# First mixer of a two-block transformer kernel: value products, selection rounds, a late sigmoid and the second output slab in another order

## The reference, cut to what matters

```python
def mixer(u, w_in, w_uk, w_uv, w_up_a, w_up_b, w_o, pos, topk):
    proj = u @ w_in                      # cut into qa ka va qb ckv krope qi ki wi ga gb
    y_a = stick_breaking(qa, ka, va)     # 8 heads: scores, log-keep sums over later keys, exp, times v
    ...
    # dsa_attention, 8 heads:
    s_idx = relu(einsum('bqhd,bkd->bqhk', qi, k_idx))       # index products
    score = einsum('bqh,bqhk->bqk', wi, s_idx)
    _, sel = lax.top_k(score, topk)                          # topk = 64 keys of each query
    p = softmax(logits of the selected keys);  y_b = p @ values
    z = sigmoid(ga) * (y_a @ w_up_a) + sigmoid(gb) * (y_b @ w_up_b)
    return z @ w_o
```

## Time and profile before

| what | value |
|---|---|
| median of 3 runs | 1602.22 us (1595.94 to 1602.30) |
| profiled execution | 1602.0 us, span 1600.2 us |
| TensorE busy | 1411.3 us, 88% |
| VectorE busy | 725.9 us, 45% |
| ScalarE busy | 522.0 us, 33% |
| GpSimd busy | 168.4 us, 11% |
| HBM read | 357.70 MB, 224 GB/s over the span |
| first mixer, from the last input slab to the last `wo` unit | about 141 to 292 us |
| expert stage | about 320 to 740 us |

### The profile page before, as it was taken

One profiled execution on the slowest core, in us unless ns is written; L12 is line 12 of the kernel. 1 busy time (PEld: TensorE's weight loads), 2 busy tenths in 40 slices (PEclk: granted clock), 3 DMA queues, 4 the chain that ended last, 5 costly groups with the idle time before them and its releaser, 6 DMA issues.

```text
span 1600.2 us, 27601 instructions
## 1 busy us (share of the span) xinstructions
PE 1411.3 (88%) x11842; PEld 1185.5 (74%) x11842; DVE 725.9 (45%) x1221; ACT 522.0 (33%) x798; POOL 168.4 (11%) x145
## 2 busy tenths in 40 slices
PE   5999888897676776776899997999999999999997
PEld 5999557764344444443697997999999887799997
DVE  4345465431121111111675566565646664566544
ACT  4354444210010000000524444344344433454442
POOL 2000002200000000000200003311124300111122
PEclk7999799798888888887899998999999999999998
DMA  7340113799999999999534540444345331354450
GB/s 310 130 189 8 73 54 139 300 410 428 428 428 429 428 428 429 428 430 427 199 143 172 211 170 3 158 182 187 114 177 210 132 145 53 127 190 171 150 180 28
DMA packets 31988, 359.98 MB, mean 225 GB/s; under 512 B 5280, under 2 KB 8352, under 8 KB 9632
## 3 DMA queue, kind: packets, MB, share of 16 engines
q1 hardware_dynamic: 31904, 358.76, 56.1%
HBM read 357.70 MB, written 1.05 MB: 224 GB/s over the span
## 4 chain that ended last, share of the span: by engine, by line
PE 68%; DMA 19%; DVE 5%; ACT 4%; issue 2%; POOL 2%; SPq 1%; ACTq 0%; DVEq 0%
PE PS L508 41%; DMA expert_w<-in_w 19%; PE PS L521 5%; PE PS L954 4%; PE PS L568 3%; PE PS L974 2%; PE PS L926 1%; SPq L387 1%; PE PS L1127 1%; DVE wl L1849 1%; ACT wh L1376 1%; PE PS L808 1%; PE PS L1321 1%; POOL UL L2543 1%; PE PS L665 1%
## 5 line engine op out<-in xcount | busy, mean ns | idle before, releaser
L1849 DVE TENSOR_TENSOR wl<-raw,wh 128x4096 fp32r<-128x4096 f32 (+2 forms) x69 | 281.4, 4078 | 215.0 <-ACT wh L1376 214.9
L1376 ACT ACTIVATE wh<-raw 128x4096 fp32r<-128x4096 f32 (+2 forms) x70 | 233.9, 3341 | 119.2 <-PE PS L508 114.0
L508 PE MATMUL PS<-UH,wh 128*128 128x272 f32 (+1 forms) x840 | 245.8, 293 | 14.0 <-DVE wl L1914 9.6
L954 PE MATMUL PS<-expert_w,XW 128*32 128x256 f32 x2048 | 161.4, 471 | 97.6 <-DMA expert_w<-in_w 97.3
L508 PE MATMUL PS<-UH,wl 128*128 128x272 f32 (+1 forms) x840 | 242.7, 289 | 0.0
L508 PE MATMUL PS<-UL,wh 128*128 128x272 f32 (+1 forms) x840 | 242.2, 288 | 0.0
L954 PEld LDWEIGHTS PS<-expert_w,XW 128*32 128x32 f32 x2048 | 74.4, 130 | 172.9 <-issue 88.6
L508 PEld LDWEIGHTS PS<-UH,wh 128*128 128x128 f32 x840 | 160.3, 191 | 16.2 <-DVE wl L1914 10.0
L508 PEld LDWEIGHTS PS<-UL,wh 128*128 128x128 f32 x840 | 160.8, 191 | 0.4
L508 PEld LDWEIGHTS PS<-UH,wl 128*128 128x128 f32 x840 | 160.5, 191 | 0.0
L2217 DVE TENSOR_TENSOR SG<-PS,SG 128x128 f32<-128x128 f32 x32 | 9.3, 291 | 284.9 <-ACT SG L1620 284.9
(11 more groups left out here) (520 smaller groups left out, 2883.5 us busy)
## 6 DMA issues: line engine op xcount, KB each, us to landing
expert_w<-in_w SPq DMA_DIRECT2D x96, 2048.0 KB, 20.7
raw<-in_up SPq DMA_DIRECT2D x22, 2048.0 KB, 7.8
raw<-in_down SPq DMA_DIRECT2D x16, 1408.0 KB, 6.1
raw<-in_ret_v SPq DMA_DIRECT2D x4, 2048.0 KB, 7.9
raw<-in_ret_gate SPq DMA_DIRECT2D x4, 2048.0 KB, 7.8
raw<-in_ret_o SPq DMA_DIRECT2D x4, 2048.0 KB, 8.5
raw<-in_ret_qk SPq DMA_DIRECT2D x3, 2048.0 KB, 7.8
raw<-in_w_in_ga SPq DMA_DIRECT2D x2, 2048.0 KB, 7.9
```

Of the source, the lines that this page charges most:

```text
L508: mm = pe.matmul(gbank(g)[:, c0:T], w[:, c:c + P], x(k)[:, c0:], start=(k == 0 and j == 0), stop=(k == nk - 1 and j == 2))
L954: mm = pe.matmul(PS[32 * j:32 * j + 32, 5 + s, 0:2 * P], XW[:, 4 * half + k, WIN * s:WIN * s + WIN], XPT[3 * s + half][:, (4 * k + j) * 2 ...
L1376: act.activation(WH[n % 2][:, 0:w], raw(n)[:, 0:w], ACT.Copy).then_inc(hi_done, 1)
L1849: dve.tensor_tensor(wl_of(n)[:, 0:w], raw(n)[:, 0:w], WH[n % 2][:, 0:w].bitcast(F32), ALU.subtract).then_inc(lo_done, 1)
```

## The change

It makes six edits, all in the first mixer:

1. On `pe`, `sb_values(0)` goes ahead of `index_products(HEADS, 4)` and `sb_values(1)` ahead of `index_products(HEADS + 4, 4)`. On `act`, `sb_high` goes ahead of `index_relu` in the same two places, and on `dve` `sb_out` ahead of `index_scores`.
2. On `dve`, six rounds of tile 0 stand between the first two pairs; `key_mask(0)` and four rounds of tile 1 ahead of `sb_softplus(3)`; `sb_out(2)`, four rounds, `key_mask(1)` and `sb_out(3)` behind it.
3. On `act`, the late sigmoid goes ahead of the four pieces of slab 12.
4. `ZT` gets four buffers in place of two, so that `dve` waits for the `ZL` of unit m - 4.
5. Slab 13 is split in four pieces on `act` and `dve`. On `dve` piece 0 stands ahead of `add_to_h(0)` and pieces 1 to 3 behind `UM` of blocks 0 to 2; the `memset` of `ZERO` goes from block 0 to block 3.
6. On `pe`, the units 4, 5 and 6 of `wo` wait for pieces 0, 1 and 2, and unit 7 for the whole slab. The piece counts that the second block waits for grow by three.

```diff
-    ZT = region("ZT", [2, T], 17408)
+    ZT = region("ZT", [4, T], 17408)
@@ pe
             pe.wait_ge(freed["act"], FREED[UNIT0["gb"] + 7][1])
+            sb_values(0)
             index_products(HEADS, 4)
-            sb_values(0)
             sb_later(1)
             sb_scores(2)
+            sb_values(1)
             index_products(HEADS + 4, 4)
-            sb_values(1)
             sb_later(2)
@@ pe
             for n in (12, 13):
-                slab_ready(n)
+                if n == 12:
+                    slab_ready(n)
                 for u in range(4):
                     m = 4 * (n - 12) + u
+                    if 4 <= m < 7:
+                        pe.wait_ge(lo_piece, 9 + u + 1)
+                    elif m == 7:
+                        slab_ready(n)
@@ pe, first_units
-                                pe.wait_ge(lo_piece, 9 + u + 1)
+                                pe.wait_ge(lo_piece, 12 + u + 1)
@@ act
             sb_log(1)
+            sb_high(0)
             index_relu(HEADS, 4)
-            sb_high(0)
             sb_weights(2)
             sb_weights(3)
             sb_log(2)
+            sb_high(1)
             index_relu(HEADS + 4, 4)
-            sb_high(1)
@@ act
+            act.activation(GB[:, 4:8, META:], GB[:, 4:8, META:], ACT.Sigmoid).then_inc(gb_sig, 1)
             for q in range(4):
                 hi_part(12, q)
-            act.activation(GB[:, 4:8, META:], GB[:, 4:8, META:], ACT.Sigmoid).then_inc(gb_sig, 1)
             for m in range(8):
                 act.wait_ge(z_done, m + 1)
-                act.activation(ZH[:, m, META:], ZT[:, m % 2, META:], ACT.Copy).then_inc(z_hi, 1)
-            hi(13)
+                act.activation(ZH[:, m, META:], ZT[:, m % 4, META:], ACT.Copy).then_inc(z_hi, 1)
+            for q in range(4):
+                hi_part(13, q)
@@ dve
             sb_softplus(1)
+            sb_out(0)
             index_scores(HEADS, 4)
-            sb_out(0)
-            for _ in range(3):
+            for _ in range(6):
                 take_best(0)
             sb_softplus(2)
+            sb_out(1)
             index_scores(HEADS + 4, 4)
-            sb_out(1)
-            for _ in range(3):
-                take_best(0)
-            sb_softplus(3)
             dve.wait_ge(dsa_in, 48)
             key_mask(0)
+            for _ in range(4):
+                take_best(1)
+            sb_softplus(3)
             sb_out(2)
-            for _ in range(3):
-                take_best(1)
-            sb_out(3)
-            for _ in range(5):
+            for _ in range(4):
                 take_best(1)
             key_mask(1)
+            sb_out(3)
@@ dve
-                if m >= 2:
-                    dve.wait_ge(z_lo, m - 1)
+                if m >= 4:
+                    dve.wait_ge(z_lo, m - 3)
@@ dve
-            lo(13)
+            lo_part(13, 0)
             for m in range(8):
                 add_to_h(UNIT0["wo"] + m, m, META)
...
-                if m == 0:
+                if m < 3:
+                    lo_part(13, m + 1)
+                elif m == 3:
                     link(dve.memset(ZERO[:], 0.0))
```

More of the change, by code:

```diff
@@ L2081, in _ @@
                     dve.wait_ge(gb_sig, 1)
-                if m >= 2:
-                    dve.wait_ge(z_lo, m - 1)
-                freeing(dve.tensor_tensor(ZT[:, m % 2, META:], gbank(g)[:, META:T], GB[:, m, META:], ALU.mult))
+                if m >= 4:
+                    dve.wait_ge(z_lo, m - 3)
+                freeing(dve.tensor_tensor(ZT[:, m % 4, META:], gbank(g)[:, META:T], GB[:, m, META:], ALU.mult))
                 dve.wait_ge(freed["dve"], FREED[g][1])
-                dve.tensor_tensor(ZT[:, m % 2, META:], ZT[:, m % 2, META:], GA[:, m, META:], ALU.add).then_inc(z_done, 1)
+                dve.tensor_tensor(ZT[:, m % 4, META:], ZT[:, m % 4, META:], GA[:, m, META:], ALU.add).then_inc(z_done, 1)
                 if m < 4:
                     lo_part(12, m)
-            lo(13)
+            lo_part(13, 0)
             for m in range(8):
@@ L2549, in _ @@
                 pool.wait_ge(z_hi, m + 1)
-                pool.tensor_tensor(ZL[:, m, META:], ZT[:, m % 2, META:], ZH[:, m, META:].bitcast(F32), ALU.subtract)\
+                pool.tensor_tensor(ZL[:, m, META:], ZT[:, m % 4, META:], ZH[:, m, META:].bitcast(F32), ALU.subtract)\
                     .then_inc(z_lo, 1)
```

## The result

The changed kernel takes **1580.68 us** (median of 4 runs, 1579.94 to 1584.37) against 1601.03 us for the kernel before, run beside it (4 runs, 1595.94 to 1602.30). The ratio is 0.9894, 95% interval 0.9860 to 0.9927: 1.1% less, some 17 us, where 19 were forecast. The profiled execution took 1584.37 us, with a span of 1582.5 us against 1600.2.

A forecast was written before the change was run, and what follows sets the result against it. TensorE carries 68% of the chain that ended last, so its pauses and the clock falls behind them counted. Terms 6.3 + 4.5 + 1.3 + 7.0 = 19.1 us, from 1602.0 us, gave 1583 us, range 1576 to 1590.

The forecast's parts named there:

- Edits 1 and 2, the order: Head pairs to first DSA maxima: value products earlier and rounds spread win 6.3 us at the clock of before.
- The 3.3 us from the rounds: End of the pairs: with rounds moved earlier, VectorE is no longer last and the maxima follow TensorE's first scores.
- The 3.0 us from the values: Two head-pair pauses: value products move into the pause, net 1.5 us for a pair, twice.
- The clock in the pauses: Two head-pair pauses, shortened to 1.9 us: one of two keeps TensorE's clock, worth 4.5 us, bounds 0 and 8.5.
- The start of the DSA steps: TensorE's pause around the first maxima all but goes, so the first gated unit runs faster: 1.3 us, bounds 0 and 2.
- Edits 3 and 4: Ahead of the output units: the wait for `ZL` goes and the first output units start 1.2 us earlier.
- Edits 5 and 6: Output units: TensorE's 3.15 us wait for `UM` goes, and with it the clock's fall, 2.6 us.
- Does it reach the end?: Expert stage moves as a whole with the chain before it; expert 0's load has over 40 us of lead.
- a loss at the experts: Rival: expert 0's lead or the load order counts, up to 6 us lost, 1589 us; chance 0.08.
- late pieces: Rival: an output unit of 4 to 7 waits for `lo_piece` in place of `UM`, 1589 us; chance 0.04.
- a late `pool`: Rival: GpSimd is last in front of the first output units and the clock falls, 1605 us, slower; chance 0.03.
- The base: Starting time for the whole kernel: the profiled execution's 1602.0 us, taken as the median of 1602.22 within 0.3 us.

The follow-up runs named there:

- the filled dispatch: Changed kernel plus 14 unused products of 256 columns on TensorE ahead of the dispatch products in the routing: 1578.16 us, ratio 0.9877.
- the filled kernel: Changed kernel plus five unused products of 432 columns ahead of the index products of steps 10 and 14 each: 1578.71 us, ratio 0.9878.
- the fully filled one: Changed kernel plus unused products in four TensorE pauses: two in the pairs, ahead of the first turning, and ahead of the dispatch: 1574.51 us, ratio 0.9863.

## Why the prediction was right, point by point

**The total.** 1583 us were forecast, within 1576 to 1590, and 1580.7 came. 19.1 us were to be won, and 17.6 us lie between the two spans. 1.5 us of them passed ahead of pair 1, in a part that the change doesn't touch (scores of pair 1 start at 158.9 instead of 160.5). So the profiles show 16 us of it, and the ratios 0.9894 and 0.9898 also 16 to 17.

**Edits 1 and 2, the order: 6.3 us.** Right in mechanism, and in size at the clock of before. The 3.3 us from the rounds: 12.6 became 9.4 or 9.5 us in every kernel that spreads them, and stayed 12.6 in every one that doesn't; 9.3 were worked out. VectorE's idle time ahead of `sb_softplus(2)` took up the rounds, as forecast: 7.53 us became 2.67. The 3.0 us from the values: the pause measured 1.74 us (1.9 forecast), `sb_high` 0.37 us (0.4 taken), and pair 1 to `sb_later(1)` went from 8.2 to 6.1 or 6.6 us (1.5 forecast). The prediction added the two edits, and the four profiles with neither, one or both show that they do add: 42.6, 39.6, 39.4 and 36.4 us. The size of the values' term hangs on the clock, though: 3.0 us where they ran at the low clock before, 1.6 us with the clock at 1.00 throughout.

**The clock in the pauses: 4.5 us, one of two kept.** Near as a size, too simple as a picture. The weak step is "as 1.9 us lies about midway between 1.35 and 2.64, I take one of the two": the length of the pause doesn't decide it. A pause of 2.64 us kept the clock once, and of the eight pauses of 1.74 us in the four profiles with this order of the pairs and no filler in them (the changed kernel twice, edits 1 and 2 alone, the filled dispatch) two kept it, in the last two kernels, the first pause each time; in both profiles of the changed kernel both pauses lost it. What also differs is how long it stayed low behind a pause: 3.4 and 13.7 us in the first profile of the changed kernel, 3.4 and 3.4 in the second, 10.2 and 6.8 us in the two with one pause kept. Against the 33.0 us of the filled kernel the low clock cost 6.6 and 3.3 us with both lost, 4.4 and 3.3 us with one lost. So a pause has no price that is either 0 or 4.5 us, it has a spread of prices. The pairs moved by 8.0 us in the profiled execution, 10.8 forecast, and by 11.3 with the second one (47.7 - 36.4); that the 10.8 lie between is in part luck. The price with the clock at 1.00 throughout was right to 0.1 us: 32.9 us worked out from the earlier trace rows, 33.0 measured once the pauses were filled. Its two parts were less exact, since the 1.9 us of values ran at the low clock too: of the 14.7 us the clock was worth 9.9 (8.5 worked out) and the order 4.8 (6.3 worked out).

The Trainium skill (TensorE: Matmul & The Clock Gate, "What's actually happening") has two levels for this clock, lifted by activity, and says that the number of slow products at a kernel's start differs from run to run. These runs agree with the two levels, and show such differences behind later pauses too: with unused products in the pause the work that took 1.56 us takes 1.01. But a busy TensorE doesn't always see its clock rise soon. In the changed kernel it worked nearly without a break behind the second pause and still was at 0.50 (columns of the earlier trace rows):

```profile
186.00:188.00 2.00, 2.00 (x10) 1.53 (x9) 0.45 (x1) 1.69 (x3) 0.00 (x0) 0.50 0.00 0
```

What decides how long the low clock stays isn't settled by these runs.

**The start of the DSA steps: 1.3 us.** The step that failed is "this pause all but goes". It shrank, but TensorE waits 1.41 us for the first probabilities at 200.30, and the first gated unit took 2.82 us in place of 1.62, as before. 0.8 us came, from another source: the low clock behind it lasted 3.4 us instead of 6.8. With the pairs filled it still took 37.8 us to `zb`; the second profile of the changed kernel, the fully filled one and two more reach 36.3, with the same pause of 1.41 us in those without a filler there and no low clock behind it. Against the 38.6 us of before the gain is thus 0.8 or 2.3 us, and the forecast 1.3 with bounds 0 and 2 stands between: the condition was wrong, and that the size came near is luck.

**Edits 3 and 4: 1.2 us.** 1.0 us in every profile with them. The table load and the sigmoid fit into the idle time with 1.00 us left in front of slab 12, as worked out. The drain of about 1.38 us that the Trainium skill names (ScalarE: Activation LUTs, "What ACT_TABLE_LOAD costs") shows neither at 233.29 nor at 254.84: the load's own 1.28 us agree with the page, the next activation starts 0.02 us behind it. By the page's figure slab 12 would have come 0.4 us late, as an estimate; it did not.

**Edits 5 and 6: 3.15 + 2.6 us.** 6.0 us in the profiled execution against 5.75, so the two terms were right for the execution they were read from. Over many runs they are 3.4 us always and 2.6 us in part of them. The timed runs of edits 5 and 6 alone, 3.8 us, say the same. The prediction took the clock's part as certain because one profile showed it; in the second profile of before the same wait of 3.17 us leaves the clock at 1.00.

**Does it reach the end?** Yes: 1280.1 and 1280.5 us from the first expert load of the loop to the end. The rivals with a loss at the experts, late pieces and a late `pool` didn't occur: TensorE waited nowhere for `lo_piece` or `ZL`, and expert 0 still has a lead of 42.2 us (load at 259.87, next one at 302.03) against 49.0 before.

**The base.** "The median of 1602.22 within 0.3 us" stood on three runs. Over 76 the median is 1597.3. From there the same sum would have given 1578.2 us, some 3 us below the 1580.7 and 1581.8 measured. So the terms were 3 us too large for an average execution, since they were read from one in which the clock fell at every place, and the base was 5 us too high for the same reason. The two errors lie on opposite sides: 5 us too high and 3 us too low leave the 2 us between 1583 and the measured time. That much of the hit is luck.

**What stays open.** Why a pause of one length sometimes keeps the clock, and why the clock sometimes comes back soon behind a pause and sometimes 10 us later. Why the filler ahead of the dispatch won 3.6 us in one kernel and nothing in the profile of the kernel with all fillers, where the interval to the load is 26.8 us, as without it. And whether the values alone bring the whole kernel more than nothing: the 3 us won at the maxima are shown, 1.1 us (-2.1 to 4.1) at the end.

## What to carry to other kernels

Ask what the engine that is last at a join itself waited for. VectorE was last at the first maxima, but its last rounds stood behind a product of TensorE, so what was won on TensorE reached the join with VectorE late (3.0 us) and with VectorE early (3.0 us). A small timed gain of a single edit doesn't show that it brings nothing: look in the profile for where it was won and where it was lost again. Read a second profile before pricing what the clock costs; a term that hangs on the clock is a range with a spread, and a base of three runs can lie 5 us off. Where TensorE must wait some microseconds between short steps, unused products into a free bank are cheap (1.24 us here, all inside the wait). In the two pauses of the pairs they bought 3.1 us, and with all four sets in place the spread was 1 us instead of 13.

## What the runs showed of the hardware

- One unchanged single-core program took 1590 to 1603 us over 76 runs, and in the two executions with a profile the clock goes with it. They are 11 us apart and differ by 10.8 us ahead of the first expert load of the loop: 1.8 before pair 1, 5.1 in the pairs, 0.3 in the DSA steps, 2.6 in the output units and 1.0 in the routing. The mean granted clock up to that load was 0.88 in the slower one and 0.93 in the other, and TensorE was busy for 281.7 and 267.6 us with the same work. The fully filled kernel keeps within 1 us in five runs.
- A wait of the same length kept the clock in one execution and lost it in another: 3.15 and 3.17 us for `UM`, and 2.64 us in the pairs.
- `ZL` on GpSimd, the same pass of 128x256, takes 0.75 us when VectorE makes z beside it, mostly from PSUM, and 1.20 us when it makes a piece of slab 12, with both inputs in SBUF (starts 241.88, 1.21 us long):

```profile
240.93 0.75 POOL L2556 TENSOR_TENSOR ZL<-ZT,ZH 128x256 fp32r<-128x256 f32 x1 [212.77 <-ACT ZH L1587]
242.49 1.21 POOL L2556 TENSOR_TENSOR ZL<-ZT,ZH 128x256 fp32r<-128x256 f32 x1 [0.81 <-ACT ZH L1587]
```

  The Trainium skill (GPSIMD Engine Reference, "1. Specifications") says that the two engines share their interfaces to SBUF and contend when a VectorE instruction has two inputs there; `lo_part` has two, and this agrees. The GpSimd steps that edit 5 now puts beside the pieces of slab 13 are slower in the same way (1.54 and 1.61 us, then 0.74 without a piece beside it), and nobody waits for them.
